# Hybrid streaming-encoder layer on one core: first loads spread over two issuing queues, small loads moved

## The reference, cut to what matters

```
h = rms_norm(x, norm_mix);  proj = h @ w_in            # 2048 x 4624
qa, ka, va, qf, kf, vf, f_logit = split(proj)
mixed = concat(sliding-window attention with sinks and rotary (qa, ka, va),
               forgetting attention (qf, kf, vf, cumsum(log_sigmoid(f_logit + b_f))))
x = x + mixed @ w_o                                    # 2048 x 2048
h = rms_norm(x, norm_ffn);  u = h @ w_up               # 2048 x 11264
c = conv_b + causal conv of width 3 over tokens (u, conv_w)
x = x + (silu(c[gate half]) * c[value half]) @ w_down  # 5632 x 2048
out = rms_norm(x, norm_final)
```

## Time and profile before

| | |
|---|---|
| runs | 1060.56, 1061.64, 1062.9 us; median 1061.64 |
| profiled execution | 1060.14 us, span of instructions 1058.3 us |
| PE busy | 1048.7 us (99% of the span) |
| DVE, ACT, POOL busy | 787.5, 626.9, 86.6 us |
| first real matmul | 9.28 us after the span's start |
| mean granted TensorE clock | 0.998 |
| DMA | 259.35 MB, mean 245 GB/s |

### The profile page before, as it was taken

How to read it: one execution, slowest core, us unless ns; L and a number is a source line. 1 busy time by engine, 2 the same in 40 slices (tenths; PEclk the granted TensorE clock), 3 DMA queues, 4 the chain that set the end, 5 groups by cost and what they waited for, 6 DMA issues and landing times.

```text
span 1058.3 us, 17826 instructions
## 1 busy us (share of the span) xinstructions
PE 1048.7 (99%) x5945; PEld 904.9 (86%) x5945; DVE 787.5 (74%) x1174; ACT 626.9 (59%) x971; POOL 86.6 (8%) x150
## 2 busy tenths in 40 slices
PE   9999999999999999999999999999999999999997
PEld 8888888888888888888888888888888888888885
DVE  5677677776555777777777877777877888877777
ACT  6956475756455555555655565555656666646663
POOL 1000000011111010111111010101111000000000
PEclk9999999999999999999999999999999999999999
DMA  9575656587888898998898898989889688887993
GB/s 300 173 231 161 186 169 176 168 256 202 246 252 231 263 250 276 253 270 235 256 275 249 267 237 272 268 256 262 249 259 258 224 294 293 274 298 266 322 316 107
DMA packets 191493, 259.35 MB, mean 245 GB/s; under 512 B 10820, under 2 KB 140580, under 8 KB 191328
## 3 DMA queue, kind: packets, MB, share of 16 engines
q1 hardware_dynamic: 173776, 215.32, 63.1%
q0 software_dynamic: 17360, 43.22, 18.7%
q10 hardware_dynamic: 320, 0.34, 0.1%
HBM read 256.73 MB, written 44.06 MB: 284 GB/s over the span
## 4 chain that ended last, share of the span: by engine, by line
PE 98%; DMA 1%; DVE 0%; SPq 0%; ACT 0%; issue 0%; DVEq 0%
PE tr_ps L1579 15%; PE pj L1579 15%; PE pj L1331 9%; PE pj L1581 8%; PE tr_ps L1581 8%; PE pj L1319 5%; PE pj L1320 5%; PE pj L1321 5%; PE pj L1333 5%; PE sc_ps L1319 4%; PE sc_ps L1321 4%; PE sc_ps L1320 4%; PE pj L1346 3%; PE pj L1348 1%; PE tr_ps L1320 1%; PE tr_ps L1321 1%
## 5 line engine op out<-in xcount | busy, mean ns | idle before, releaser
L889 DVE TENSOR_TENSOR split<-raw,split 128x1024 fp32r<-128x1024 f32 x266 | 321.7, 1223 | 146.7 <-ACT split L578 141.4
L578 ACT ACTIVATE split<-raw 128x1024 fp32r<-128x1024 f32 x260 | 270.7, 1057 | 97.2 <-PE pj L1581 28.7
L1579 PE MATMUL tr_ps<-act_split,split 128*128 128x512 f32 x704 | 245.5, 392 | 0.0
L1579 PE MATMUL pj<-act_split,split 128*128 128x512 f32 x704 | 245.0, 391 | 0.0
L1581 PE MATMUL pj<-act_split,split 128*128 128x256 f32 x704 | 197.6, 281 | 0.0
L1581 PE MATMUL tr_ps<-act_split,split 128*128 128x256 f32 x704 | 197.6, 281 | 0.0
L1168 DVE TENSOR_TENSOR split<-raw,split 128x1024 fp32r<-128x1024 f32 (+1 forms) x124 | 137.2, 1136 | 37.9 <-ACT split L834 35.7
L834 ACT ACTIVATE split<-raw 128x1024 fp32r<-128x1024 f32 (+1 forms) x124 | 119.5, 987 | 69.0 <-PE sc_ps L1321 31.9
L1579 PEld LDWEIGHTS tr_ps<-act_split,split 128*128 128x128 f32 x704 | 131.8, 187 | 28.5
L1579 PEld LDWEIGHTS pj<-act_split,split 128*128 128x128 f32 x704 | 131.7, 187 | 28.6
L1331 PE MATMUL pj<-act_split,split 128*128 128x512 f32 x416 | 147.1, 398 | 0.0
(11 more groups left out here) (240 smaller groups left out, 1512.6 us busy)
## 6 DMA issues: line engine op xcount, KB each, us to landing
raw<-w_up SPq DMA_DIRECT2D x176, 512.0 KB, 6.0
raw<-w_in SPq DMA_DIRECT2D x72, 512.0 KB, 3.8
raw<-w_down SPq DMA_DIRECT2D x68, 512.0 KB, 5.6
t_dram<-w_down POOLq DMA_DIRECT2D x60, 512.0 KB, 6.5
raw<-t_dram SPq DMA_DIRECT2D x40, 512.0 KB, 5.7
raw<-w_o SPq DMA_DIRECT2D x32, 512.0 KB, 5.7
t_dram<-t_dram POOLq DMA_DIRECT2D x40, 256.0 KB, 6.0
raw<-w_down SPq DMA_DIRECT2D x20, 256.0 KB, 5.6
```

What stands on the lines that cost most here:

```text
L578: ins = act.activation(hi[:, slot, 0:TILE], raw[:, slot, 0:TILE], ACT.Copy)
L889: dve.tensor_tensor(lo[:, slot, 0:n], raw[:, slot, 0:n], hi[:, slot, 0:n].bitcast(F32), ALU.subtract).then_inc(lo_done, 1)
L1579: pe.matmul(up_banks[v][b], wh[:, c, b * P:(b + 1) * P], act_both(k), start=k == 0, stop=False, skip_group_check=True)
```

## The change

WARM goes from 9 to 8. x0m1 is issued from ACT's queue ahead of ident; va0, g0 and g1 follow ident on ACT's queue and leave SP's. norm_ffn moves from ACT's queue to POOL's and, with POOL's seven small DMAs behind it, waits until x quarter 1 has landed (`d_x[1]` at 32). Its 16 gains are no longer turned with norm_mix but with the conv weights, by one more PE transpose and one more ACT copy at t = 9. The splits of tile 0 are interleaved with the evacuations: blocks 0, 1, chunk 0, block 2, chunk 1, block 3, chunks 2, 3, on ACT and on DVE.

```diff
-WARM = 9
+WARM = 8
@@ sync
             def load_x(c):
-                for m in range(MT):
+                for m in range(1 if c == 0 else MT):
                     sp.dma_start(nat[:, m, c * 512:(c + 1) * 512],
                                  x[0, m * P:(m + 1) * P, c * 512:(c + 1) * 512]).then_inc(d_x[c], 16)
@@
-                sp.dma_start(with_gates(raw, va_slot)[:, :, 0:256], win[kt][:, :, COL_VA:COL_VA + 256]).then_inc(d_w[va_slot], 16)
-                sp.dma_start(with_gates(raw, va_slot)[:, :, 256:VA_COLS], win[kt][:, :, COL_F:COL_F + NH]).then_inc(d_w[va_slot], 16)
+                if kt > 0:
+                    sp.dma_start(with_gates(raw, va_slot)[:, :, 0:256], win[kt][:, :, COL_VA:COL_VA + 256]).then_inc(d_w[va_slot], 16)
+                if kt > 1:
+                    sp.dma_start(with_gates(raw, va_slot)[:, :, 256:VA_COLS], win[kt][:, :, COL_F:COL_F + NH]).then_inc(d_w[va_slot], 16)
@@ gpsimd
             pool.memset(ones[:], 1.0).then_inc(ones_s, 1)
+            pool.wait_ge(d_x[1], 32)
+            pool.dma_start(rows[KB:2 * KB, 0], norm_ffn.rearrange("a (b p) -> (a b) p", p=P)).then_inc(d_cnv, 16)
@@ scalar
+            act.dma_start(nat[:, 1, 0:512], x[0, P:2 * P, 0:512]).then_inc(d_x[0], 16)
             act.dma_start(ident[:], ident_c).then_inc(d_id, 16)
-            act.dma_start(rows[KB:2 * KB, 0], norm_ffn.rearrange("a (b p) -> (a b) p", p=P)).then_inc(d_nrm, 16)
+            act.dma_start(with_gates(raw, 0)[:, :, 0:256], win[0][:, :, COL_VA:COL_VA + 256]).then_inc(d_w[0], 16)
+            for kt in range(2):
+                act.dma_start(with_gates(raw, 2 * kt)[:, :, 256:VA_COLS], win[kt][:, :, COL_F:COL_F + NH]).then_inc(d_w[2 * kt], 16)
@@
-            act.activation(cst[:, 0:2 * KB], pj[:, 3, 0:2 * KB], ACT.Copy).then_inc(cst_c, 1)
+            act.activation(cst[:, 0:KB], pj[:, 3, 0:KB], ACT.Copy).then_inc(cst_c, 1)
@@ (the same in the vector block, with lo)
                 input_hi(c)
-                if c % 2 == 1:
+                if c > 0:
                     split_hi_part(0, c - 1)
-                    split_hi_part(0, c)
+            split_hi_part(0, 3)
@@
-                        act.activation(cst[:, 2 * KB:384], tr_ps[:, 1, 128:480], ACT.Copy).then_inc(cst_c, 1)
+                        act.activation(cst[:, 2 * KB:384], tr_ps[:, 1, 128:480], ACT.Copy)
+                        act.activation(cst[:, KB:2 * KB], tr_ps[:, 1, 480 + KB:512], ACT.Copy).then_inc(cst_c, 1)
@@ tensor
-                    pe.wait_ge(d_nrm, 32)
-                    pe.transpose(pj[:, 3, 0:2 * KB], rows[0:2 * KB, 0, :], ident[0:2 * KB, 0:2 * KB]).then_inc(cst_t, 1)
+                    pe.wait_ge(d_nrm, 16)
+                    pe.transpose(pj[:, 3, 0:KB], rows[0:KB, 0, :], ident[0:KB, 0:KB]).then_inc(cst_t, 1)
@@
-                        pe.wait_ge(d_cnv, 64)
+                        pe.wait_ge(d_cnv, 80)
+                        pe.transpose(tr_ps[:, 1, 480:512], rows[0:2 * KB, 0, :], ident[0:2 * KB, 0:2 * KB])
```

More of the change, by code:

```diff
@@ L912, in _ @@
                 input_lo(c)
-                if c % 2 == 1:
+                if c > 0:
                     split_lo_part(0, c - 1)
-                    split_lo_part(0, c)
+            split_lo_part(0, 3)
             split_lo(1, 1)
```

## The result

The changed kernel takes 1067.12 us (median of six runs, 1066.39 to 1068.72), the kernel before 1061.72 (six runs, with three new ones). The ratio is 1.0053 with a 95% interval of 1.0040 to 1.0066, so 4.2 to 7.0 us slower. I had forecast 1064.6 and at most 1066.9: the direction was right, half of the loss was missing.

A forecast was written before the change was run, and what follows sets the result against it. PE was taken as the bound, its start set by g0's landing. +2.9 us for g0 and +0.1 for the rest, added to the 1061.64 median, gave 1064.6; range 1060.9 to 1066.9, likeliest case 1063.4 to 1065.7.

The forecast's parts named there:

- the clock: Rival at tile 0: PE's idle stretch drops it to 1.2 GHz, 2.0 us more, 1066.6; chance 0.10.
- the likeliest case: Opening loads: the two queues share engines packet for packet, clock unchanged; 1064.6, 1063.8 to 1065.3; chance 0.52.
- The landing of g0: Opening load on ACT's queue: g0 lands at 11.1 us instead of 8.19, +2.9 us, between +2.1 and +3.6.
- The transpose at t = 9: One more PE transpose with the conv weights, costing 0.38 / 4 = 0.1 us on the path.
- g0 sets the start, and ka0 and x1 overtake it packet by packet: Opening: g0 arrives last and fixes PE's start at 12.2 us; ka0 and x1, at equal packets, are complete before it.
- POOL's traffic: Opening: moving POOL's small transfers later was credited with 1.3 us of the 16 DMA engines' time.
- behind 1.6 MB: Opening of the kernel before: g0's landing, 5.6 us after its issue, was read as waiting on 1.6 MB, not an issue slot.
- Costed at nothing: ACT's five early DMAs, late sinks and conv weights, ACT's extra copy: hidden; interleaved splits: 0, or 0.1 us if cover is gone.
- Equal bytes: Rival in the opening: queues get equal bytes, g0 +0.9 us; with issue order 1062.6 to 1063.1, joint chance 0.19.
- ACT's queue unhindered: Rival in the opening: SP's loads leave ACT's queue its bandwidth, 0.71 us won less 0.1, 1061.0; chance 0.19.
- It doesn't do what it says: Rival in the opening: ident, behind x0m1, lands at 5.4 to 5.8, so turning x starts unchanged; no separate chance.
- Nothing is given back: After PE's start: ka0 and x1 land earlier, but no idle PE hides a late start, so the whole delay stays.

The follow-up runs named there:

- loads_back: The changed kernel with va0, g0 and g1 issued by SP again, ahead of ka0: 1062.65 us, ratio 1.0006 to the kernel before.
- gates_sp: The changed kernel with only g0 and g1 issued by SP again, va0 still on ACT's queue: 1062.31 us, ratio 1.0006 to the kernel before.
- sp_holds: The changed kernel with SP waiting for va0 and g0 to land before issuing ka0 and all behind it: 1064.62 us, ratio 1.0024 to the kernel before.
- pool_late: The kernel before with one edit, POOL waiting for x quarter 1 before its seven small DMAs: 1060.84 us, ratio 0.9992.
- norm_last: The kernel before with norm_ffn moved to t = 9, its added transpose behind the four conv transposes: 1063.49 us, ratio 1.0012.
- act_only: The kernel before with one more ACT copy of 16 columns at t = 9, result unused: 1062.17 us, ratio 1.0000.
- norm_late: The kernel before with only norm_ffn moved: loaded by POOL without a wait, turned and copied with the conv weights at t = 9: 1063.57 us, ratio 1.0018.

## Why the prediction was right in sign and wrong in size

By the two profiles the loss was 6.3 us, where the sum had 3.0. Three of its terms were too small. The largest miss, and the step that failed, is the clock: the likeliest case let PE stand idle for 3.4 us and put the clock at nothing, and the runs show 1.53 us for it. The landing of g0 was sized 0.86 us too short. The transpose at t = 9 was put at 0.1 and cost 0.9, by a change of pace that no term had. With the clock alone in the sum the range would have held the result.

**g0 sets the start, and ka0 and x1 overtake it packet by packet: right.** g0 landed last, ka0 and x1 before it, at 8.4 and 10.4 (my count had them at equal packets before g0), and loads_back, gates_sp and sp_holds each removed the delay in another way. The rule taken from a stretch of 1.5 us in which 128 packets stood against 107 held to 1% from 7 us to g0's landing, 1190 to 1181. In the microseconds before it was looser, 460 to 374.

**The size of that term: too small by 0.86 us, mostly by my own choice.** The sum gave 11.7 for g0's landing, and I took 11.1, "nearer to the measured x1m1", on a backlog that I argued might shrink. It landed at 11.96. The backlog didn't shrink. When g0 was complete, 3.07 MB had passed, and the count had 2.58 (2520 KB); before, when x1m1 was complete, 3.00 MB had passed, for 2.21 counted and 0.21 of POOL's. PE's start: 12.2 forecast, 13.04 measured, +3.76 for +2.9. Inside the sum another part was off: POOL's traffic was credited with 1.3 us up to x1; pool_late shows about 0.9. One reading beside the sum was wrong too: g0 before wasn't "behind 1.6 MB". The loads issued ahead of it are 1.1 MB, and 1.74 MB in all had passed when it landed.

**The clock: a rival that belonged to the main case.** I gave it 0.10, priced at 2.0 us, and wrote that PE would stand idle for 3.4. It idled 2.98 us and the clock fell, at 14.1, for 3.4 us; measured price 1.53 us. The condition that I had written (the idle stretch grows sevenfold) followed from my likeliest case; it had no separate chance. Priced with it, 1064.6 would have been 1066.6, and the upper end of that case 1065.3 + 2.0 = 1067.3, above the 1067.12. Missed too: one warm-up less, warm-ups that ended sooner since the clock rose at 3.9 us, and a later ident made the first idle stretch longer (1.65 us for 0.59), and the clock was low from 7.3 to 10.7 as well, which g0's wait hid. That the longer stretch brought this first fall about is likely, not shown: in loads_back and gates_sp the clock rose at 4.3 and 4.5 us, PE idled 1.15 and 0.91 us, and it didn't fall.

The Trainium skill, "TensorE: Matmul & The Clock Gate", Part 1, says that an idle TensorE falls back to half rate. The trace now agrees: the granted clock was 0.50 from 14.1 us on, 1.1 us after a wait of 3.0 us had ended.

**norm_ffn turned at t = 9: 0.1 us forecast, 0.9 measured.** The added transpose itself took 0.18. What I hadn't in any term is that the stretch from the conv transposes on becomes 0.7 us longer (six kernels without it 33.69 or 33.70, seven with it ahead 34.40 or 34.41, norm_last 34.67). I costed an instruction on a fully busy engine by its own duration alone.

**Costed at nothing, and right:** the five DMAs on ACT's queue (its table load started at 3.52, against a first copy at 6.91), the late sinks and conv weights (PE and DVE show no wait on them), the interleaved splits (no idle PE within tile 0), ACT's extra copy (act_only 1.0000).

**The other rivals.** Equal bytes is out by 644 to 645 and by gates_sp; ACT's queue unhindered is out by the changed kernel itself. "It doesn't do what it says" came true in part: ident, behind x0m1, landed at 6.01 for 4.95, and the turning of x started 0.27 us later.

**"Nothing is given back": wrong by 0.2 us.** The wait of before on ka0 (PE's first matmul with keys at 13.39, 0.14 after DVE's 13.25) was in the chain without showing as idle PE, and ka0's earlier landing took it away.

The terms together: 3.76 + 1.53 to the turning of quarter 1, 0.3 given back until 46.6 us, 0.18 + 0.71 at t = 9, 0.4 later: 6.3 us. The 0.4 is a change of pace that the change doesn't explain. One attention pass took 51.8 or 52.4 us in kernels with the same instructions there (pool_late 51.9, then 52.4), so differences of this size come from one execution to the next. From the first turned block to the end the fourteen profiles took 981.4 to 983.9 us, in no order that follows the edits, and the 981.9 of the changed kernel is near the low end. At t = 9 it is otherwise: there the pace followed the transpose in all fourteen. What makes a PE loop take the one or the other pace stays open.

## What to carry to other kernels

The order of issue on one queue is close to a priority: before the change SP's loads landed in that order, but for x1m0, which came 0.15 us ahead of ka0. A second queue gives it up: what is needed first shares, packet for packet, with everything that the other queue holds, and small rows lose most. Move to the second queue only what would otherwise be served ahead of the critical load, or small-row loads beside a large one, never the critical load with kilobyte rows running against its 64-byte ones. This is advice against a loss: no kernel here with a load on the second queue was measurably faster than the kernel before.

When a forecast makes PE wait, price the clock in the same case. And on an engine that is 99% busy an added instruction should be measured together with the loop behind it.

## What the runs showed of the hardware that I had not expected

- Two queues share the 16 DMA engines one packet for one packet over 2 us and 1289 packets (644 and 645), though one's were of 64 B and the other's of 1 KB: 0.04 MB against 0.65 MB. In each 0.05 us some 16 packets of each start, so the queues take turns after every row.
- The granted clock fell to 0.50 while PE was working on tile 0, 1.1 us after its wait of 3.0 us had ended, not during the wait, and stayed there for 3.4 us. When it first rose differed between profiles: at 3.9 to 6.4 us in eight of them, at 9.8 to 12.5 in five, at 19.5 in one. norm_late and norm_last are the same program until t = 9, and in them it rose at 10.7 and 5.5, with second warm-ups of 2.77 and 1.51 us.
- One PE transpose of 0.17 us more, on either side of four others, made the 34 us behind it 0.7 to 0.8 us longer, the same to 0.01 us in all seven kernels that have it ahead. A pair of matmuls then starts every 0.353 us for 0.347. Every kernel has stretches at both paces.
- POOL's small transfers took 46% of the DMA engines for 1.5 us with 0.01 MB, and with the other stretches 1.3 us of their time in all. Without them the loads beside them landed 0.1 (g0), 0.6 (va0), 0.9 (x1m1) and 1.5 us (ka0) earlier. A queue's share of the engines' time isn't what its removal gives back to each load.
